# Output projection of a hybrid diffusion layer: the context tile's modulation rows loaded ahead into free down-projection slots

## The reference

```
sh1, sc1, g1, sh2, sc2, g2 = split(mod, 6)          # mod_ctx for context, mod_lat for latent tokens
h = rmsnorm(x, g_pre_mix) * (1 + sc1) + sh1
mixed = concat(gated MLP, attention, S5 scan of h @ w_in) @ w_out     # output projection
x = x + g1 * rmsnorm(mixed, g_post_mix)
h = rmsnorm(x, g_pre_ffn) * (1 + sc2) + sh2
x = x + g2 * rmsnorm(moe(h), g_post_ffn)            # router, top 8 of 64 experts, 1 shared expert
```

## Time and profile before

| | |
|---|---|
| median of 3 runs | 1442.24 us (1441.34 to 1446.01) |
| profiled execution | 1441.92 us, span from first to last instruction 1440.2 us |
| TensorE matmuls | busy 91% of the span, 1315.2 us |
| VectorE, ScalarE, GpSimd | 39%, 24%, 22% |
| mean granted TensorE clock | 0.941 of 2.4 GHz |
| `route` up to the last logits | 442 to 547 us |
| shared expert and routing tables | 547 to 608 us |
| experts | 610 to 1363 us |
| `combine` | from 1367 us |

### The profile page before, as it was taken

How to read it: one execution, slowest core, us unless ns; L and a number is a source line. 1 busy time by engine, 2 the same in 40 slices (tenths; PEclk the granted TensorE clock), 3 DMA queues, 4 the chain that set the end, 5 groups by cost and what they waited for, 6 DMA issues and landing times. The chain is left out here.

```text
span 1440.2 us, 26978 instructions
## 1 busy us (share of the span) xinstructions
PE 1315.2 (91%) x8994; PEld 751.4 (52%) x8994; DVE 564.0 (39%) x1701; ACT 339.5 (24%) x675; POOL 322.9 (22%) x388
## 2 busy tenths in 40 slices
PE   4998999898778959999999999999999999999766
PEld 2543644766654534455555555555555555555422
DVE  1282457286331434433333333333333333333158
ACT  4121010165112221122222222222222222222111
POOL 4021140130001000023333332323323333233101
PEclk9899799978589988999999999999999999999978
DMA  9865533553016150282498498989999898683195
GB/s 352 242 155 183 181 136 144 164 159 116 27 59 268 76 232 16 91 332 74 164 394 354 179 396 336 415 341 400 393 383 417 344 417 332 264 337 127 40 423 233
DMA packets 90153, 349.10 MB, mean 242 GB/s; under 512 B 22661, under 2 KB 27924, under 8 KB 62592
## 3 DMA queue, kind: packets, MB, share of 16 engines
q1 hardware_dynamic: 68208, 300.31, 54.2%
q0 software_dynamic: 21040, 46.67, 8.8%
q10 hardware_dynamic: 864, 1.57, 0.3%
HBM read 484.32 MB, written 46.87 MB: 369 GB/s over the span
## 5 line engine op out<-in xcount | busy, mean ns | idle before, releaser
L1906 PE MATMUL banks<-rings,hT 128*64 128x256 f32 x3712 | 420.0, 379 | 1.9 <-ACT hT L1796 1.2
L1906 PEld LDWEIGHTS banks<-rings,hT 128*64 128x64 f32 x3712 | 261.4, 137 | 189.4 <-issue 67.9
L1930 PE MATMUL banks<-downs,hT 128*64 128x512 f32 x928 | 222.0, 600 | 0.9 <-issue 0.9
L1769 POOL DMA_INDIRECT h<-h2D,toks x117 | 118.2, 1011 | 453.9 <-DVE kept L1833 433.7
L1796 ACT ACTIVATE hT<-banks 128x512 f32<-128x512 f32 x116 | 69.3, 597 | 377.7 <-PE banks L1893 377.7
L1782 POOL DMA_INDIRECT yD<-hT,dest x116 | 118.0, 1018 | 131.5 <-ACT hT L1810 129.0
L1866 DVE COPY hT<-banks 128x128 f32<-128x128 f32 x116 | 33.8, 292 | 254.9 <-PE banks L1917 254.9
L1810 ACT ACTIVATE hT<-banks,gain 128x512 f32<-128x512 f32 x116 | 79.7, 687 | 179.3 <-PE banks L1930 179.3
L1930 PEld LDWEIGHTS banks<-downs,hT 128*64 128x64 f32 x928 | 56.1, 138 | 68.4 <-issue 68.4
L1823 DVE COPY info<-wparts 128x20 bf16 x118 | 21.3, 181 | 153.7 <-issue 152.6
L1893 PE MATMUL banks<-ident,h 128*128 128x128 f32 x464 | 76.1, 287 | 0.0
(11 more groups left out here) (452 smaller groups left out, 1512.3 us busy)
## 6 DMA issues: line engine op xcount, KB each, us to landing
rings<-w_e_gate SPq DMA_DIRECT2D x116, 1024.0 KB
rings<-w_e_up SPq DMA_DIRECT2D x116, 1024.0 KB
downs<-w_e_down SPq DMA_DIRECT2D x116, 1024.0 KB
rings<-w_ada SPq DMA_DIRECT2D x12, 2048.0 KB, 11.8
rings<-yD SPq DMA_DIRECT2D x8, 2048.0 KB, 17.2
rings<-w_in SPq DMA_DIRECT2D x4, 2048.0 KB, 12.6
rings<-matD SPq DMA_DIRECT2D x3, 2048.0 KB, 14.9
matD<-rings SPq DMA_DIRECT2D x2, 2048.0 KB
```

The lines of the kernel that those rows point to most:

```text
L1769: pool.indirect_dma_start(out=xg[u], out_offset=None, in_=k.h2D, bounds_check=2 * TOK - 1, oob_is_err=False, in_offset=bass.IndirectOffset ...
L1906: last = pe.matmul(bank[par][h * SB:(h + 1) * SB, 0:F], lhsT=lhsT, rhs=w[:, (h * KD + kk) * F:(h * KD + kk + 1) * F], start=(kk == 0), sto ...
L1930: last = pe.matmul(bank[4 + par][h * SB:(h + 1) * SB, :], lhsT=hidT[par][:, kk, :], rhs=down[:, kk * D + h * 512:kk * D + (h + 1) * 512], ...
```

## The change

SP loads the context rows at the start of the block, behind the five tiles of `x` and ahead of the router's weights: the gate into the first half of `dn[3]`, the shift into its second half, the scale into the first half of `dn[0]`. VectorE reads them from there for tile 4, and the latent rows stay where they are. GpSimd's wait and its three loads go. The loads of expert weights into `dn[0]` and `dn[3]` move behind the gate and up loads and wait for the last `h2`.

```
+    lat_rows = (gate_b[:, :], shift_b[:, :], scale_b[:, :])
+    ctx_rows = (k.dn[3][:, 0:D], k.dn[3][:, D:2 * D], k.dn[0][:, 0:D])
...
         for t in range(NT):
             sp.dma_start(k.x1[:, t, :], x_src[t]).then_inc(x_in, 16)
+        for tile, g in zip(ctx_rows, (2, 3, 4)):
+            sp.dma_start(tile, k.modD[0, g].partition_broadcast(P)).then_inc(ctx_b, 16)
         sp.dma_start(wr[:, :, :], a["w_router"][0].rearrange("(p k) e -> p k e", k=KD)).then_inc(wr_in, 16)
...
         sp.wait_ge(mix_ready, NT)
         load_gu(sp, k, a, 0, 0)
+        load_gu(sp, k, a, 2, 2)
+
+        sp.wait_ge(h2_ready, NT)
         load_down(sp, k, a, 0, 0)
-        load_gu(sp, k, a, 2, 2)
         load_down(sp, k, a, 2, 2)
...
         for t in range(NT):
-            if t == CTX_T:
-                pool.wait_ge(h2_ready, CTX_T)
-                for tile, g in ((gate_b, 2), (shift_b, 3), (scale_b, 4)):
-                    pool.dma_start(tile[:, :], k.modD[0, g].partition_broadcast(P)).then_inc(ctx_b, 16)
             pool.wait_ge(h2_ready, t + 1)
...
             if t == CTX_T:
                 dve.wait_ge(ctx_b, 48)
+            gate_r, shift_r, scale_r = ctx_rows if t == CTX_T else lat_rows
```

More of the change, by code:

```diff
@@ L1366, in _ @@
         for t in range(NT):
[L1367 to L1370, removed]
             pool.wait_ge(h2_ready, t + 1)
@@ L1431, in _ @@
                 half = slice(h * 512, (h + 1) * 512)
-                last = stt(tmp[:, half], bank[2 * (t % 2) + h][:, :], rstd[:, t, 0:1], gate_b[:, half], ALU.mult, ALU.mult)
+                last = stt(tmp[:, half], bank[2 * (t % 2) + h][:, :], rstd[:, t, 0:1], gate_r[:, half], ALU.mult, ALU.mult)
             v(last)
@@ L1441, in _ @@
             v(stt(spread, x.rearrange("p (q k) -> p q k", k=KD), rstd[:, t, 1:2],
-                  scale_b[:, :].rearrange("p (q k) -> p q k", k=KD), ALU.mult, ALU.mult))
-            tt(spread, spread, shift_b[:, :].rearrange("p (q k) -> p q k", k=KD), ALU.add).then_inc(h2_ready, 1)
+                  scale_r.rearrange("p (q k) -> p q k", k=KD), ALU.mult, ALU.mult))
+            tt(spread, spread, shift_r.rearrange("p (q k) -> p q k", k=KD), ALU.add).then_inc(h2_ready, 1)
         def hidden(t):
```

## The result

The changed kernel takes **1432.34 us** (median of 4 runs, 1430.60 to 1434.02) against 1441.99 us; the ratio is 0.9928, 95% interval 0.9915 to 0.9940. (The ratios here are estimated over the runs and differ a little from the quotient of two medians.) The forecast was 1434.6 us, within 1431.0 to 1437.8. The profiled execution took 1434.02 us, with a span of 1432.1 us. That is 8.1 us less than the span before.

What follows compares the result with a forecast made beforehand. The prediction took TensorE to be held by tile 4's chain, where VectorE waits for the context rows' DMA. Its terms summed to 7.65 + 0 = 7.65 us off the median of 1442.24: 1434.6 us, range 1431.0 to 1437.8.

Steps and rivals of the forecast that it cites:

- The wait that goes: VectorE's sum of tile 4 would no longer wait for the context rows' DMA, beginning at 524.04 instead of 531.69: 7.65 us gained.
- Rows read from the down slots: Tile 4's chain reads gate, shift and scale from the down-projection slots: put at nothing, 0.1 us either way.
- Three issues on SP: Context loads behind x delay later issues by 1.4 us and their data by 4.2 us; enough cover, so no cost.
- the 3.0 us: Claimed slack between the last x tile's landing at 456.5 and VectorE's first sum at 459.52, ahead of tile 0.
- Two loads later: Down-projection loads of slots 0 and 2 wait for the last h2, until 533.1; cover of 74 us, so no cost.
- The clock: TensorE's half clock around tile 4's transposes stays as before: put at nothing, bounded by 3.8 us gained and 1.7 us lost.
- The tax: Time TensorE loses at half clock in tile 4's transposes, the logits and the shared expert's start: 3.8 us in all.
- B: Rival: TensorE's clock stays at full or comes back early, up to 3.8 us more gained, 1430.8 us; chance 0.07.
- C: Rival: loads of the experts' weights swallow the gain in the expert stage, 1442.2 us, no change; chance 0.09, half-way cases included.
- D: Rival: x lands late, so the tiles start late and the kernel is 5.2 us slower, 1447.4 us; chance 0.03.
- E: Rival: another condition holds tile 4, so the change doesn't do what it says, 1442.2 us; chance 0.01.
- the forecast's own range: For the whole kernel, 1432.5 to 1436.8 us around the forecast alone, without rivals; the forecast's chance was 0.80.

Runs made afterwards that it cites:

- the filled kernels before: The kernel before plus 34 or 16 extra, unused matmuls in TensorE's wait ahead of tile 4's transposes: 1449.83 us (ratio 1.0066) and 1438.81 us (0.9975).
- the one with the work of tile 0: The kernel before with the shared expert's gate and up matmuls of tile 0 run ahead of tile 4's transposes: 1433.84 us, ratio 0.9947.
- two filled kernels: The one with the fall at 521.8 us is the changed kernel plus 16 extra, unused matmuls, 1435.67 us; the text does not identify the other.
- the filling: Extra, unused matmuls in TensorE's wait: 8 in the changed kernel, 1430.26 us; 16 in the kernel before, 1438.81 us; unfilled kernel before, 1442.02 us.
- the second and the third comparison: The changed kernel rerun without edit against the kernel before: 1433.67 against 1443.46 us (0.9929); on another chip 1433.17 against 1442.02 us (0.9936).

## Why the prediction was right, point by point

- *The wait that goes, 7.65 us.* Right in place and size: 7.58, 9.18 - 16.75 = -7.57 and 9.17 - 16.75 = -7.58 in three profiles. The sum of tile 4 follows ScalarE; nothing else was late. But all three are set against one profile of the kernel before, and there the wait is not as steady: in three other profiles in which GpSimd's rows land beside 6 MB (the filled kernels before and the one with the work of tile 0) the sum comes 7.89, 8.23 and 8.26 us behind the squares, for 7.68. The wait that goes is thus 7.6 to 8.2 us, 7.9 in the mean.
- *Rows read from the down slots, 0.1 us.* Right: L1444 and L1446 take 1.96 and 1.89 us.
- *Three issues on SP, nothing.* Right for the time: x landed as before. The cover ahead of tile 0 was thinner than the prediction said, since the 3.0 us hung on a half clock at the stage's start.
- *Two loads later, nothing.* Right, and shown alone (ratio 0.9997). They were issued at 531.02; the write of tile 4's h2, issued beside them, landed after 8.9 us instead of 4.0, and the first gather, 60 us later, did not wait for it.
- *The clock, nothing, from +3.8 to -1.7 us.* Right that it is down behind either wait, at 0.50. The tax was sized at 3.8 us and measured at 3.7 to 5.0. The reason given, a fall 0.8 us into the idle time, was too simple: in the changed kernel the fall came 2.7, 0.2 and 2.8 us behind the last matmul, in the two variants of the kernel before with SP's loads put off 0.15 us before its end, and in two filled kernels while the filling ran (at 521.8 and 522.7 us). The later return cost 1.36 us in the first profile (11.5 us after the transposes began for 8.8), 1.39 in the third (11.6) and nothing in the second (9.0; section of 69.37 us). So the return moved from run to run, and the 8.8 us of before do not hold for the changed kernel. The 6 to 12 us named for it in the prediction were an estimate.
- *The rivals.* B: the clock did not stay up. C: the expert stage has 749.19 us for 749.18. D: x was not late. E: the chain did what the diff says.
- *The sum.* The time lies 2.3 us below the forecast and inside the range. It lies just below the forecast's own range (1432.5 to 1436.8), in the room that was left for B, which did not happen. So the mechanism was right, the size of the saving short by 1 to 2 us, and that the time is still inside the range is partly luck. The saving was forecast as 7.65 us and measured as 9 to 10 in three comparisons. What the difference is, is not settled. It is not the order of the loads as far as that was tested (0.9997), and hardly the clock behind the wait (the filling gives about the same in both kernels). The other profiles point to two places. The wait of the kernel before is 0.3 us longer in their mean than in the one profile that the prediction read. And the section up to the squares is 1.7 us shorter in three of seven profiles with the rows ahead, 0.7 us in the mean. That makes 7.9 + 0.7 = 8.6 us, which lies within the intervals of the second and the third comparison (from 7.9 and 7.4 us on) and at the edge of the first (from 8.7); whether the 0.7 is chance, no run tells. The runs agree that the changed kernel spends less time at half clock: the mean granted clock is 0.9409 over 41 runs of before (span 1440.8) and 0.9452 over 15 of the changed kernel (1431.1), or 170 and 157 us at half clock. Of the 13 us less, about 8 would be the shorter wait itself, where half clock costs nothing; the other 5 would be 2 to 3 us of work, by estimate.

## What to carry to other kernels

A load that replaces a buffer's last use is late by construction; read whether the wait behind it ends on the DMA, and take the same step of the previous tile as the measure of what will be left. Then ask what the waiting engine could do in the rest of the wait: here 7 us of work put into the remaining 8 us were worth 9 to 10 us, as much again as the load itself. And check whether the loads that crowd out the late one could simply stand behind it: one wait gave 7.2 us.

## What the runs showed of the hardware

Three loads of 512 KB took 13.0 and 13.6 us from the last issue beside 6 and 4 MB of expert weights, and 7.6 us with these held back. In the kernels with a wait of 8 to 16 us ahead of tile 4's transposes, TensorE's granted clock fell from 1.00 to 0.50 between 0.15 us before the end of the last matmul and 4.1 us behind it. In the three kernels in which filling or work left 1.4, 1.4 and 1.0 us of that wait, with 1.2 us of waiting behind the transposes, it fell in the last logits (at 535.8 and 543.2 us) or 0.3 us behind them (536.75 us). In three it fell for 3.4 us while the filling or the work put ahead ran (from 520.5, 521.8 and 522.7 us), and in one it stayed at 1.00 over 29.40 us of filling. With a wait of 8 us or more the return came 8.6 to 11.6 us after TensorE took up work, and the work behind the wait, up to the experts, took 3.7 to 5.0 us longer than the 65.64 us of two kernels in which the granted clock was 1.00.
